# One decoder step on one core: the decode requests' heads move beside the delta rule, and prompt attention gets a block of its own

## The chip, the cores and the metric

The kernel runs on one core of a Trainium2 chip. The metric is the device time of one launch in microseconds (us). TensorE (PE) multiplies matrices; VectorE (DVE), ScalarE (ACT) and GpSimd (POOL) work element by element; SyncE (SP) issues most DMAs. Each engine takes its own instructions in the order in which they are written, and semaphores hold an engine until another has done something. TensorE runs at 1.2 or 2.4 GHz; the profile's "PEclk" is the granted share of 2.4 GHz.

## What is computed

One layer of a hybrid decoder for a prompt of 2048 tokens and for 8 decode requests of one token each, with 8192 earlier tokens of each request in a paged cache. The 1024-wide mix is made of two groups of four heads of 128.

```python
proj = jnp.einsum('btd,de->bte', rms_norm(x, norm_mix), w_in)
o_gdn, gdn_buf, gdn_s = gdn_branch(qkv, z, a, b, ...)   # gated delta rule, state 128x128 per head
o_dsa = dsa_fn(l, q, k, v, iq, ik, iw)                  # attention over the 256 best tokens
x = x + jnp.einsum('bte,ed->btd', concat(o_gdn, o_dsa), w_out)
...

def dsa_attend(q_pos, q, iq, iw, ik_all, gather_kv, n_sel, rel_bias):
    rel = relu(einsum('bthd,bsd->bths', iq, ik_all))
    score = einsum('bths,bth->bts', rel, iw)              # 8 index heads of 64
    _, sel = lax.top_k(score, n_sel)                      # 256 tokens
    k_sel, v_sel = gather_kv(sel)
    logits = einsum('btkgd,btskd->btkgs', qg, k_sel) * HEAD_DIM ** -0.5 + bias
    p = softmax(where(valid, logits, -inf))
    o = einsum('btkgs,btskd->btkgd', p, v_sel)
```

The layer ends with a causal convolution of three tokens over an up projection and a gated down projection.

Both parts do this: the prompt part for 2048 queries, the sample part for 8 requests against 8193 keys each, with one step of the delta rule for each request.

## The kernel before

The program is a row of blocks; a block ends on all engines before the next begins. `project`, `keys` and `channels` project the tokens; `channels` also makes the prompt's choice of 256 tokens and leaves it in DRAM as `left`. Then come, in this order, the five blocks that the change touches:

- `rule_and_attention` (names `mid_`): the delta rule for the prompt (`Delta`) and the prompt's attention (`Attention`), written into one stream for each engine. Before the rule, `Gates` prepares the decays.
- `delta_step` (`dstep_`): one step of the rule for the 8 requests, 32 states of 128x128.
- `step_select` (`pick_`): scores of 8192 cached index keys of each request, then a search for the 256th best score bit by bit, in 33 rounds.
- `step_slots` (`slot_`): turns the chosen tokens into lists of cache rows by one-hot matmuls.
- `step_attend` (`satt_`): gathers keys and values by indirect DMA and attends.

After them `mix`, `ffn_up` and `ffn_down` close the layer; they are not changed.

**The rule.** `Delta` takes the 16 chunks of 128 tokens as 8 pairs, `b` = 0 and 1 (buffers `A[b]`, `B[b]` in PSUM). A pair has an early stage (`sums`, `rows`, turns, `gram`), then 6 levels of a triangular inverse, then a late stage (`wt`, `vnew`, `kv`, `kvo`, output). A level writes on TensorE 4 products of `atm` and `x` (L2517) for each chunk, which ACT copies to `y` (L2610), and 4 products for `x` (L2526) and 4 for `xt` (L2529), which DVE subtracts (L2748, L2750). In the last level the product for `x` is left out. An f32 product is two MATMULs in the trace, so the six levels of a pair are 96 + 80 + 96 = 272 MATMULs of 64 columns, and a whole pair has 472.

**Attention.** `Attention` goes through 64 steps, a tile of 128 queries times a head. Step s does q·k in groups of 512 keys (L2177) with the mask added by a bf16 product (L2179), ACT copies each group out of PSUM (L2254), DVE adds the near bias (L2344) and takes the maximum (L2345), ACT takes the exponential (L2268). Two steps later TensorE turns the probabilities (L2192), ACT copies them (L2263), and TensorE multiplies them by v (L2228). q·k has two PSUM buffers, the turned probabilities have one. The tiles 0 to 3 have one group, 12 to 15 have four.

**What sets the order.** Each stage of the rule calls `side.spend(w)` with a weight that is written down by hand. `Beside` then advances the other stream until its share of its own total weight is as large as the rule's share. So the two are interleaved evenly by weight on every engine, and nothing at run time changes that order. The weights of the rule add up to 104.2 for a pair.

## Time and profile before

| what | us |
|---|---|
| median of 3 runs (4658.73 to 4661.22) | 4660.68 |
| the profiled execution's own time | 4658.32 |
| its span, first to last instruction | 4657.1 |
| block of rule and attention (1262 to 2343) | 1081 |
| four blocks of the sample part (2343 to 2823) | 480 |

The span is the execution that the rows below come from; it is 3.6 us under the median. The mean granted clock over it was 0.884. In a stretch the busy columns say for how long an engine had an instruction in work, with the count in brackets. A busy TensorE can be busy at half clock, so its busy time is read together with PEclk.

### The profile page before, as it was taken

To read this page: it belongs to the slowest core of one execution; us is meant where nothing else is said; L and a number is where in the kernel's file an instruction comes from. 1 tells how busy PE (TensorE), PEld (TensorE's weight loads), DVE (VectorE), ACT (ScalarE), POOL (GpSimd) and SP (SyncE) were. 2 spreads that over 40 slices of the span, in tenths; PEclk is the share of its full clock that TensorE was granted. 3 is DMA by queue.
4 is the path that set the end of the run, shared out by engine and by line. 5 is a ranking of instruction groups with operands and counts; after the bars stand their busy time and mean duration, and the time that the engine had idled before them with its cause. 6 is when DMAs were issued, how large, how long until landed. Compare 5 with 4: busy or idle time off the path is not lost. (4 is left out here: it accounts for less than half of the span.)

```text
span 4657.1 us, 51408 instructions
## 1 busy us (share of the span) xinstructions
PE 3985.0 (86%) x19290; PEld 3182.1 (68%) x19290; DVE 2136.5 (46%) x4206; ACT 1528.2 (33%) x2435; POOL 691.7 (15%) x547
## 2 busy tenths in 40 slices
PE   7788888888588888988859348989999999979999
PEld 4444454445287777877749334459999999958877
DVE  5538989898834433433322651224444444430200
ACT  2125565565434444544402001112222222221211
POOL 0100000000032222221200020111111111124443
PEclk9889899999768889989955557999999999989999
DMA  2242222120211111101031013311111111145433
GB/s 90 82 105 58 73 53 64 44 63 23 72 57 36 49 36 39 32 21 33 3 119 72 0 37 109 108 56 44 48 55 36 55 36 55 45 127 178 129 105 117
DMA packets 287233, 298.37 MB, mean 64 GB/s; under 512 B 33999, under 2 KB 231503, under 8 KB 282026
## 3 DMA queue, kind: packets, MB, share of 16 engines
q1 hardware_dynamic: 271822, 256.80, 19.2%
q0 software_dynamic: 2112, 20.97, 1.2%
q10 hardware_dynamic: 13120, 18.25, 1.2%
q8 instruction: 107, 1.75, 0.2%
q14 instruction: 72, 0.59, 0.0%
HBM read 202.16 MB, written 94.10 MB: 64 GB/s over the span
## 5 line engine op out<-in xcount | busy, mean ns | idle before, releaser
L530 PE MATMUL chan_p_g<-ht,chan_w 128*128 128x412 f32 (+1 forms) x1760 | 678.3, 529 | 62.7 <-ACT chan_flat L578 33.7
L1568 PE MATMUL up_p_g<-ht_high,up_wh 128*128 128x412 f32 (+1 forms) x1760 | 617.7, 351 | 0.3 <-POOL up_wl L1614 0.3
L1568 PE MATMUL up_p_g<-ht_high,up_wl 128*128 128x412 f32 (+1 forms) x1760 | 615.2, 350 | 0.0
L1568 PE MATMUL up_p_g<-ht_low,up_wh 128*128 128x412 f32 (+1 forms) x1760 | 615.2, 350 | 0.0
L530 PEld LDWEIGHTS chan_p_g<-ht,chan_w 128*128 128x128 f32 x1760 | 341.9, 197 | 310.5 <-issue 230.7
L1586 ACT ACTIVATE up_pre<-up_p_g 128x412 f32<-128x412 f32 (+1 forms) x220 | 113.6, 516 | 748.9 <-PE up_p_g L1568 748.9
L1948 ACT ACTIVATE chan_signed<-chan_sc,chan_trial 128x512 bf16<-128x512 f32 (+6 forms) x224 | 305.2, 1362 | 148.4 <-DVE chan_trial L2003 127.7
L1568 PEld LDWEIGHTS up_p_g<-ht_high,up_wh 128*128 128x128 f32 x1760 | 331.5, 188 | 1.9 <-issue 0.7
L1568 PEld LDWEIGHTS up_p_g<-ht_low,up_wh 128*128 128x128 f32 x1760 | 331.4, 188 | 1.2
L1568 PEld LDWEIGHTS up_p_g<-ht_high,up_wl 128*128 128x128 f32 x1760 | 331.2, 188 | 0.5
L1638 DVE TENSOR_SCALAR up_acc<-up_pre,up_taps 128x2048 f32<-128x2048 f32 x44 | 59.3, 1347 | 574.9 <-ACT up_pre L1586 574.9
L1989 DVE TENSOR_SCALAR_CACHE_REDUCE chan_tie<-chan_sc,chan_trial 128x384 bf16<-128x384 f32 (+6 forms) x224 | 316.2, 1412 | 7.5
L1806 PE MATMUL down_p_y<-down_wl,down_ah 128*128 128x512 f32 x704 | 274.4, 390 | 0.0
L1805 PE MATMUL down_p_y<-down_wh,down_ah 128*128 128x512 f32 x704 | 274.3, 390 | 0.0
L1807 PE MATMUL down_p_y<-down_wh,down_al 128*128 128x512 f32 x704 | 274.2, 389 | 0.0
L1924 PE MATMUL chan_p_sc<-ik,chan_iq 128*128 128x512 f32 (+3 forms) x304 | 185.9, 615 | 100.8 <-ACT chan_r L1943 90.6
L1777 POOL TENSOR_TENSOR down_al<-down_a,down_ah 128x1024 fp32r<-128x1024 f32 x88 | 211.7, 2406 | 359.0 <-ACT down_ah L1751 359.0
L1390 PE MATMUL mix_p_y<-mix_w,mix_m 128*128 128x512 f32 x544 | 238.9, 598 | 19.0 <-DMA mix_m<-scratch_mix 19.0
L1614 POOL TENSOR_TENSOR up_wl<-up_w,up_wh 128x1024 fp32r<-128x1024 f32 x44 | 128.8, 2928 | 839.6 <-ACT up_wh L1580 831.1
L1943 ACT ACTIVATE chan_r<-chan_p_sc 128x512 f32<-128x512 f32 (+3 forms) x304 | 159.7, 544 | 221.7 <-PE chan_p_sc L1925 115.4
L1751 ACT ACTIVATE down_ah<-down_a 128x1024 fp32r<-128x1024 f32 x88 | 93.4, 1061 | 385.9 <-PE down_p_y L1807 373.9
L1390 PEld LDWEIGHTS mix_p_y<-mix_w,mix_m 128*128 128x128 f32 x544 | 103.2, 192 | 143.3 <-issue 143.3
(521 smaller groups left out, 6962.2 us busy)
## 6 DMA issues: line engine op xcount, KB each, us to landing
down_a<-scratch_act SPq DMA_DIRECT2D x88, 512.0 KB, 3.6
scratch_act<-up_acc SPq DMA_DIRECT2D x22, 1028.0 KB, 5.2
up_w<-in_w_up SPq DMA_DIRECT2D x44, 512.0 KB, 6.4
chan_iq<-scratch_iq SPq DMA_DIRECT2D x28, 512.0 KB, 7.1
scratch_qkv<-chan_acc SPq DMA_DIRECT2D x12, 1028.0 KB, 4.6
mid_raw<-scratch_qkv SPq DMA_DIRECT2D x16, 768.0 KB, 5.4
chan_w<-in_w_in SPq DMA_DIRECT2D x22, 512.0 KB, 4.4
proj_x<-in_x_prompt SPq DMA_DIRECT2D x16, 512.0 KB, 3.6
```

Source lines behind the costliest of these rows:

```text
L530: last = pe.matmul(p_g[u % BANKS][:, 0:cols.stop - cols.start], weights[:, k, :], K.ht[:, k, cols], start=(k == 0), stop=(k == KD - 1))
L1390: last = pe.matmul(p_y[b][:, half, :], m[b][:, k, :], w[:, k, half * 512:(half + 1) * 512], start=(k == 0), stop=(k == KD - 1))
L1568: last = pe.matmul(p_g[u][:, 0:cols.stop - cols.start], wp[s][:, k, :], hp[:, k, cols], start=(k == 0 and m == 0), stop=(k == KD - 1 and m ...
L1614: pool.tensor_tensor(wl[s][:, :, :], w[s][:, :, :], wh[s][:, :, :].bitcast(F32), ALU.subtract).then_inc(s_wl[s], 1)
L1777: pool.tensor_tensor(al[t % RING][:, :, :], a[t % RING][:, :, :], ah[t % RING][:, :, :].bitcast(F32), ALU.subtract)\
L1805: pe.matmul(bank[0:m, :], hi, wh[:, f, :], start=(f == 0), stop=False)
L1806: pe.matmul(bank[0:m, :], hi, wl[:, f, :], start=False, stop=False)
L1807: last = pe.matmul(bank[0:m, :], lo, wh[:, f, :], start=False, stop=(f == NF - 1))
L1924: pe.matmul(out, self.iq[b][:, 0, h, :], self.K.ik2[:, cols], start=True, stop=False)
L1943: act.activation(self.r[n % self.RING][:, 0:width], self.p_sc[n % 2][:, 0:width], ACT.Relu).then_inc(S["relu"], 1)
L1948: act.activation(self.signed[:, 0:nk], self.sc[1][:, 0:nk], ACT.Sign, scale=-1.0, bias=self.trial[:, 1:2].bitcast(F32), accum_out=self.sig ...
L1989: last = dve.tensor_scalar(self.tie[:, 0:na], self.sc[0][:, 0:na], trial[:, 0:1].bitcast(F32), None, ALU.is_ge, ALU.add, accum_out=count[: ...
```

## The change

The four blocks of the sample part are gone as blocks. A class `Sample` writes the same work as a stream of steps with weights for each engine, in five parts: scoring (64 units of 4 transposes and 4 products), rule step (21 steps), search (35), slots (13) and attention (26). `heads` puts this stream beside the rule, over all eight pairs, where prompt attention stood; the prompt's attention, unchanged in its order, follows in a block of its own (`att_`) with nothing beside it. The sample stream weighs 6 + 171.6 + 42 + 84 + 65 + 62.4 = 431. The index pages of the first two pairs of requests are fetched before the rule starts. Slots are built in halves of 64 columns. Otherwise the sample part computes what it computed, in as many units and rounds.

```diff
-    def total(self):
+    def total(self, pairs):
...
-        return self.N * (early + (LEVELS - 1) * (self.W_YV + self.W_PROD) + late)
+        return 2 * len(pairs) * (early + (LEVELS - 1) * (self.W_YV + self.W_PROD) + late)
...
-    def tensor(self, pe, side):
+    def tensor(self, pe, side, pairs):
...
-        for j in range(self.N // 2):
+        for j in pairs:
...
+class Sample:
...
+    W_PREP, W_SCORE, W_RULE, W_SEARCH, W_SLOT, W_ATTEND = 3.0, 2.6, 2.0, 2.4, 5.0, 2.4
...
+    RULE_STEPS, SLOT_STEPS, ATTEND_STEPS = 21, 13, 26
+
+    def total(self):
+        return (2 * self.W_PREP + (self.UNITS + 2) * self.W_SCORE + self.RULE_STEPS * self.W_RULE + (self.ROUNDS + 2) * self.W_SEARCH
+                + self.SLOT_STEPS * self.W_SLOT + self.ATTEND_STEPS * self.W_ATTEND)
...
+    def tensor(self, pe):
+        yield from self.prepare_tensor(pe)
+        yield from self.score_tensor(pe)
+        yield from self.rule_tensor(pe)
+        yield from self.search_tensor(pe)
+        yield from self.slot_tensor(pe)
+        yield from self.attend_tensor(pe)
...
+    def vector(self, dve):
+        yield from self.prepare_vector(dve, step)
+        yield from self.score_vector(dve)
+        yield from self.rule_vector(dve, step)
+        yield from self.search_vector(dve, step)
+        yield from self.slot_vector(dve, step)
+        yield from self.attend_vector(dve, step)
...
+    def score_tensor(self, pe):
+        K, S, bank = self.K, self.S, self.bank
+        for step in range(self.UNITS + 2):
+            u = step
+            if u < self.UNITS:
+                i = u // self.PER
+                if u % self.PER == 0:
+                    pe.wait_ge(K.s_page[i % 2], i // 2 * 16 + 16)
+                if u >= 2:
+                    pe.wait_ge(S["copy"], u - 1)
+                for k in range(4):
+                    last = pe.transpose(bank[u % 2][:, k * P:(k + 1) * P], self.pages[i % 2][:, u % self.PER * 4 + k, :], K.ident[:, :])
+                last.then_inc(S["turn"], 1)
+            u = step - 1
+            if 0 <= u < self.UNITS:
+                if u == 0:
+                    pe.wait_ge(S["bd"], 1)
+                    pe.wait_ge(S["wread"], 1)
+                pe.wait_ge(S["copy"], u + 1)
+                if u >= 2:
+                    pe.wait_ge(S["mul"], u - 1)
+                for k in range(4):
+                    last = pe.matmul(bank[2 + u % 2][:, k * 32:(k + 1) * 32], self.turned[u % 2][:, k, :],
+                                     self.bd[:, u // self.PER, :, :, :].rearrange("p k q h -> p (k q h)"), start=True, stop=True)
+                last.then_inc(S["score"], 1)
+            yield self.W_SCORE
...
+    def search_tensor(self, pe):
+        K, S, bank = self.K, self.S, self.bank
+        for m in range(self.ROUNDS):
+            pe.wait_ge(S["row"], m + 1)
+            pe.matmul(bank[0][:, 0:PAIRS], K.halves[:, :], self.row[:, :], start=True, stop=True).then_inc(S["total"], 1)
...
+    def search_vector(self, dve, step):
...
+        def tally(level):
+            dve.tensor_tensor(nhit[:, :], sn[:, :], level, ALU.is_ge)
+            step(dve.tensor_tensor(hit[:, :, :], s[:, :, :], level.unsqueeze(2).broadcast_to(wide), ALU.is_ge))
+            dve.tensor_reduce(row[:, :], hit[:, :, :], AX.X, ALU.add).then_inc(S["row"], 1)
+
+        def too_few(m):
+            dve.wait_ge(S["total"], m + 1)
+            step(dve.tensor_tensor(count[:, :], bank[0][:, 0:PAIRS], nhit[:, :], ALU.add))
+            step(dve.tensor_scalar(miss[:, :], count[:, :], float(NSEL), None, ALU.is_lt))
...
+            tally(trial[:, :].bitcast(F32))
+            yield self.W_SEARCH
+            too_few(31 - bit)
+            step(dve.scalar_tensor_tensor(out=trial[:, :], in0=miss[:, :], scalar=bit, in1=other[:, :],
+                                          op0=ALU.logical_shift_left, op1=ALU.bitwise_xor))
...
+def heads(nc, K, ins, outs):
+
+
+    with phase(nc, "rule") as (c_rule, stack_rule):
+        rule = Delta(c_rule, K, ins["gdn_out_norm"].rearrange("l (p o) -> (l p) o", o=1), outs["p_gdn"].rearrange("h k v -> k h v"))
+        with phase(nc, "step") as (c, stack):
+            few = TILES * GH
+            gate = Gates(c, K, ins["gdn_a_log"], ins["gdn_dt_bias"], rule.A[0][:, 0, 0:few], rule.B[0][:, 0, 0:few])
+            sample = Sample(c, K, ins, outs)
+            pairs = range(NT // 2)
+            beside = lambda stream: Beside(stream, sample.total(), rule.total(pairs))
+            block = open_block(nc, stack, c)
+
+            @block.sync
+            def _(sp):
+                gate.sync(sp)
+                rule.sync(sp, beside(sample.sync(sp)), pairs)
+                sample.finished(sp)
+
+            @block.tensor
+            def _(pe):
+                gate.tensor(pe)
+                rule.tensor(pe, beside(sample.tensor(pe)), pairs)
+
+            @block.scalar
+            def _(act):
+                gate.scalar(act)
+                rule.scalar(act, beside(sample.scalar(act)), pairs)
+
+            @block.gpsimd
+            def _(pool):
+                gate.gpsimd(pool)
+                sample.begin(pool)
+                pool.wait_ge(gate.S["g"], 1)
+                rule.gpsimd(pool, beside(sample.gpsimd(pool)), pairs, gate.S["ready"])
+
+            @block.vector
+            def _(dve):
+                gate.vector(dve)
+                dve.wait_ge(gate.S["ready"], 1)
+                rule.vector(dve, beside(sample.vector(dve)), pairs)
+
...
+    with phase(nc, "att") as (c, stack):
         att = Attention(c, K)
-        beside = lambda stream: Beside(stream, att.total(), rule.total())
+        alone = lambda stream: Beside(stream, att.total()).rest()
...
         def _(pe):
-            gate.tensor(pe)
-            rule.tensor(pe, beside(att.tensor(pe)))
+            alone(att.tensor(pe))
...
-                rule_and_attention(nc, K, ins["gdn_a_log"], ins["gdn_dt_bias"], ins["gdn_out_norm"].rearrange("l d -> (l d)"), outs)
-                delta_step(nc, K, ins["state_gdn"].rearrange("l b h k v -> (l b) h k v"),
-                           ins["gdn_out_norm"].rearrange("l d -> (l d)"), dict(outs, s_gdn=outs["s_gdn"].rearrange("(b h) k v -> b h k v", h=GH)))
...
-                step_select(nc, K, ins["cache_idx_k"].rearrange("l n p d -> (l n) p d"), ins["page_table"])
...
-                step_slots(nc, K, ins["page_table"])
-                step_attend(nc, K, ins["cache_k"], ins["cache_v"], ins["q_norm"].rearrange("l d -> (l d)"))
...
+                heads(nc, K, ins, outs)
```

**TensorE in the levels.** Before, the start of the levels of a rule pair; `mid_p_a` names are prompt attention, which sits between the rule's pieces:

```order
L2517 MATMUL mid_p_A<-mid_x,mid_atm 128x64 x4
L2177 MATMUL mid_p_a_l<-mid_a_kt,mid_a_qg 128x512
L2179 MATMUL mid_p_a_l<-mid_a_left,mid_a_shut 128x512
L2517 MATMUL mid_p_A<-mid_x,mid_atm 128x64 x4
L2526 MATMUL mid_p_B<-mid_y,mid_xt 128x64 x4
L2529 MATMUL mid_p_B<-mid_xt,mid_y 128x64 x4
L2192 MATMUL mid_p_a_t<-ident,mid_a_lg 128x128 x4
L2177 MATMUL mid_p_a_l<-mid_a_kt,mid_a_qg 128x512
L2179 MATMUL mid_p_a_l<-mid_a_left,mid_a_shut 128x512
L2526 MATMUL mid_p_B<-mid_y,mid_xt 128x64 x4
```

The same place in the first pair now (line numbers are those of the changed file); `step_` names are the sample part, here its scoring:

```order
L1866 MATMUL rule_p_A<-rule_x,rule_atm 128x64 x8
L1875 MATMUL rule_p_B<-rule_y,rule_xt 128x64 x4
L1878 MATMUL rule_p_B<-rule_xt,rule_y 128x64 x4
L2515 MATMUL step_p_s<-ident,step_pages 128x128 x4
L2526 MATMUL step_p_s<-step_bd,step_turned 128x32 x4
L1875 MATMUL rule_p_B<-rule_y,rule_xt 128x64 x4
L1878 MATMUL rule_p_B<-rule_xt,rule_y 128x64 x4
L1866 MATMUL rule_p_A<-rule_x,rule_atm 128x64 x8
L2515 MATMUL step_p_s<-ident,step_pages 128x128 x4
```

Where wide products of attention stood between the rule's 64-column products there are now 4 transposes and 4 products of 32 columns.

**VectorE in the search.** Before, a round of the search is written alone, in `step_select`:

```order
L973 TENSOR_REDUCE pick_row<-pick_hit 128x4
L975 TENSOR_TENSOR pick_count<-pick_p_c,pick_nhit 128x4
L987 TENSOR_SCALAR pick_miss<-pick_count 128x4
L988 SCALAR_TENSOR_TENSOR pick_trial<-pick_miss,pick_other 128x4
L983 TENSOR_SCALAR pick_other<-pick_trial 128x4
L971 TENSOR_TENSOR pick_nhit<-pick_sn,pick_trial 128x4
L972 TENSOR_TENSOR pick_hit<-pick_s,pick_trial 128x512
```

Now it stands between the rule's subtractions of the levels:

```order
L2099 TENSOR_TENSOR rule_x<-rule_x,rule_p_B 128x128x2
L2101 TENSOR_TENSOR rule_xt<-rule_xt,rule_p_B 128x128x2
L2699 TENSOR_TENSOR step_count<-step_p_s,step_nhit 128x4
L2700 TENSOR_SCALAR step_miss<-step_count 128x4
L2715 SCALAR_TENSOR_TENSOR step_trial<-step_miss,step_other 128x4
L2709 TENSOR_SCALAR step_other<-step_trial 128x4
L2693 TENSOR_TENSOR step_nhit<-step_sn,step_trial 128x4
L2694 TENSOR_TENSOR step_hit<-step_s,step_trial 128x512
L2695 TENSOR_REDUCE step_row<-step_hit 128x4
L2099 TENSOR_TENSOR rule_x<-rule_x,rule_p_B 128x128x2
L2101 TENSOR_TENSOR rule_xt<-rule_xt,rule_p_B 128x128x2
```

and on TensorE the product that the round waits for stands between the rule's products:

```order
L1866 MATMUL rule_p_A<-rule_x,rule_atm 128x64 x8
L1875 MATMUL rule_p_B<-rule_y,rule_xt 128x64 x4
L1878 MATMUL rule_p_B<-rule_xt,rule_y 128x64 x4
L2678 MATMUL step_p_s<-step_row,halves 128x4
L1875 MATMUL rule_p_B<-rule_y,rule_xt 128x64 x4
L1878 MATMUL rule_p_B<-rule_xt,rule_y 128x64 x4
L1866 MATMUL rule_p_A<-rule_x,rule_atm 128x64 x4
L2678 MATMUL step_p_s<-step_row,halves 128x4
```

A round's count (L2678 on TensorE) waits for the DVE row above (L2695) that is written at the same place of the rule, and the rule's next products stand behind it.

**TensorE in the block of attention alone.** Now, a step of a tile with two groups of keys:

```order
L1523 MATMUL att_p_a_l<-att_a_kt,att_a_qg 128x512
L1525 MATMUL att_p_a_l<-att_a_left,att_a_shut 128x512
L1538 MATMUL att_p_a_t<-ident,att_a_lg 128x128 x4
L1523 MATMUL att_p_a_l<-att_a_kt,att_a_qg 128x256
L1525 MATMUL att_p_a_l<-att_a_left,att_a_shut 128x256
L1538 MATMUL att_p_a_t<-ident,att_a_lg 128x128 x2
L1574 MATMUL att_p_a_o<-att_a_v,att_a_pt 128x128 x6
```

The same pieces as before follow one another without the rule's between them.

## Rows read from the trace of the kernel before

**Rows 1.** Busy time by stage: the rule block, then the sample blocks.

```profile
core 0 of [0], span 4657.1 us
core 0: us, PE busy (x) PEld busy (x) DVE busy (x) ACT busy (x) POOL busy (x), PEclk, DMA share, GB/s
1262.00:2343.00 1081.00, 920.63 (x6086) 803.63 (x6086) 409.01 (x926) 477.30 (x837) 257.79 (x291) 0.86 0.13 37
2343.00:2823.00 480.00, 278.13 (x1625) 259.45 (x1625) 191.18 (x560) 48.67 (x83) 38.48 (x42) 0.51 0.16 54
```

**Rows 2.** The same columns: scoring, slots, pair 1, its levels, levels of pair 3.

```profile
2417.00:2590.00 173.00, 160.70 (x774) 158.88 (x774) 39.84 (x154) 38.27 (x64) 1.88 (x2) 0.50 0.19 76
2681.00:2746.00 65.00, 28.50 (x522) 27.46 (x522) 51.18 (x95) 0.00 (x0) 3.44 (x5) 0.61 0.02 3
1281.80:1424.40 142.60, 123.08 (x669) 113.35 (x669) 53.08 (x152) 59.58 (x124) 36.82 (x40) 0.68 0.17 50
1320.90:1396.80 75.90, 73.28 (x364) 69.03 (x365) 21.54 (x63) 24.59 (x56) 22.59 (x27) 0.57 0.10 29
1589.90:1650.20 60.30, 55.51 (x407) 49.38 (x407) 23.59 (x46) 24.12 (x45) 20.97 (x26) 0.92 0.06 16
```

**Rows 3.** TensorE groups in the levels of pair 1.

```profile
L2529 PE MATMUL mid_p_B<-mid_xt,mid_y 128*128 128x64 f32 x96 | 19.4, 370 | 0.0
L2517 PE MATMUL mid_p_A<-mid_x,mid_atm 128*128 128x64 f32 x96 | 19.3, 376 | 4.5 <-DVE mid_xt L2739 4.5
L2526 PE MATMUL mid_p_B<-mid_y,mid_xt 128*128 128x64 f32 x80 | 17.2, 389 | 0.0
```

**Rows 4.** TensorE in order of time, levels of pair 1: start, length.

```profile
1341.88 1.91 PE L2526 MATMUL mid_p_B<-mid_y,mid_xt 128*128 128x64 f32 x8
1343.58 1.92 PE L2529 MATMUL mid_p_B<-mid_xt,mid_y 128*128 128x64 f32 x8
```

**Rows 5.** The same view in the levels of pair 3.

```profile
1629.22 1.08 PE L2177 MATMUL mid_p_a_l<-mid_a_kt,mid_a_qg 128*128 128x512 f32 x2
1630.13 0.38 PE L2179 MATMUL mid_p_a_l<-mid_a_left,mid_a_shut 128*128 128x512 bf16 x1
1630.35 1.00 PE L2526 MATMUL mid_p_B<-mid_y,mid_xt 128*128 128x64 f32 x8
1631.19 1.06 PE L2529 MATMUL mid_p_B<-mid_xt,mid_y 128*128 128x64 f32 x8
1632.08 0.61 PE L2192 MATMUL mid_p_a_t<-ident,mid_a_lg 128*128 128x128 f32 x4
1632.53 1.06 PE L2228 MATMUL mid_p_a_o<-mid_a_v,mid_a_pt 128*128 128x128 f32 x8
```

**Rows 6.** Groups while the sample part scores: names, count, busy, mean ns, idle.

```profile
L894 PE MATMUL pick_p_x<-pick_bd,pick_turned 128*128 x512 | 112.7, 386 | 0.0
L884 PE MATMUL pick_p_t<-ident,pick_pages 128*128 128x128 f32 x256 | 69.1, 429 | 9.9 <-DMA pick_pages<-in_cache_idx_k,pick_pid 9.9
```

**Rows 7.** All engines in order of time, one search round.

```profile
2641.42 0.59 PE L901 MATMUL pick_p_c<-pick_row,halves 128*128 128x4 f32 x2 [2.25 <-DVE pick_row L973]
2642.04 0.16 DVE L975 TENSOR_TENSOR pick_count<-pick_p_c,pick_nhit 128x4 f32<-128x4 f32 x1 [0.68 <-PE pick_p_c L901]
...
2644.25 0.58 PE L901 MATMUL pick_p_c<-pick_row,halves 128*128 128x4 f32 x2 [2.25 <-DVE pick_row L973]
```

**Rows 8.** The tile of attention's logits: count, duration min/median/max in ns.

```profile
L2254 ACT ACTIVATE mid_a_lg<-mid_p_a_l,mid_a_rq x160: 353/687/703, 1289.3 to 2298.3; 128x512 f32<-128x512 f32 x112, 128x128 f32<-128x128 f32 x16, 128x256 f32<-128x256 f32 x16, 128x384 f32<-128x384 f32 x16
L2344 DVE TENSOR_TENSOR mid_a_lg<-mid_a_lg,near x64: 281/419/1059, 1294.3 to 2301.7; 128x256 f32<-128x256 f32 x60, 128x128 f32<-128x128 f32 x4
L2345 DVE TENSOR_REDUCE mid_a_bias<-mid_a_lg x64: 286/1287/2287, 1294.7 to 2302.1; 128x1 f32<-128x128 f32 x4, 128x1 f32<-128x256 f32 x4, 128x1 f32<-128x384 f32 x4, 128x1 f32<-128x512 f32 x4
L2268 ACT ACTIVATE mid_a_lg<-mid_a_lg,mid_a_bias x64: 401/1202/2004, 1295.0 to 2304.4; 128x128 f32<-128x128 f32 x4, 128x256 f32<-128x256 f32 x4, 128x384 f32<-128x384 f32 x4, 128x512 f32<-128x512 f32 x4
```

**Rows 9.** ScalarE groups of the whole block: count, busy us, mean ns.

```profile
L2263 ACT ACTIVATE mid_a_pt<-mid_p_a_t 128x512 f32<-128x512 f32 (+3 forms) x160 | 84.7, 530 | 88.2 <-PE mid_p_a_t L2192 87.2
...
L2298 ACT ACT_TABLE_LOAD x16 | 20.5, 1283 | 0.3
```

More of the change, by code:

```diff
@@ L2570, in tensor, with scalar @@
         side.rest()
-    def scalar(self, act, side):
+    def scalar(self, act, side, pairs):
         S, A, B, st = self.S, self.A, self.B, self.st
-        for j in range(self.N // 2):
+        for j in pairs:
             for b in range(2):
@@ L2632, in scalar, with gpsimd @@
         side.rest()
-    def gpsimd(self, pool, side, ready):
+    def gpsimd(self, pool, side, pairs, ready):
         K, S = self.K, self.S
-        pool.memset(K.state[:, :, :], 0.0).then_inc(S["zero"], 1)
-        for j in range(self.N // 2):
+        if 0 in pairs:
+            pool.memset(K.state[:, :, :], 0.0).then_inc(S["zero"], 1)
+        for j in pairs:
             for b in range(2):
@@ L2682, in gpsimd, with vector @@
         side.rest()
-    def vector(self, dve, side):
+    def vector(self, dve, side, pairs):
         K, S, A, B, st = self.K, self.S, self.A, self.B, self.st
-        step = Chain(dve, S["step"])
-        dve.wait_ge(S["gain"], 16)
-        dve.wait_ge(S["zero"], 1)
-        for j in range(self.N // 2):
+        step = Chain(dve, S["step"], self.steps)
+        if 0 in pairs:
+            dve.wait_ge(S["gain"], 16)
+            dve.wait_ge(S["zero"], 1)
+        for j in pairs:
             for b in range(2):
@@ L2783, in vector @@
         side.rest()
+        self.steps = step.n
 class Gates:
@@ L2880, in _ @@
         def _(sp):
-            gate.sync(sp)
-            rule.sync(sp, beside(att.sync(sp)))
+            alone(att.sync(sp))
             att.finished(sp)
```

1320 lines of the change are left out of this document (701 added, 619 removed).

## The prediction, made before the changed kernel was run

> **What bounds the kernel now.** Read the busy time by stage first [rows 1]. The stretch that the change rewrites is 1081 us of rule and prompt attention and 480 us of sample part, 1561 of the span's 4657.1. In the first block TensorE is busy for 921 of 1081 us at a mean granted clock of 0.86, and no other engine for more than 477. So TensorE is the bound there. In the sample blocks no engine is: TensorE has 278 us, DVE 191, and they wait for one another. That is the 480 us the change can win, and it wins them only if TensorE has room beside the rule for 278 us.
>
> Read the clock next, since TensorE's busy time hangs on it. In the levels of pair 3, with attention of two key groups between them, the granted clock is 0.92 and 407 MATMULs take 60.3 us. In the levels of pair 1, where attention's tiles are at most four blocks wide, it is 0.57, and 364 MATMULs take 75.9 us, though TensorE is busy for 73.3 of them [rows 2]. While the sample part scores, TensorE is busy for 160.7 of 173 us and the clock is 0.50 throughout. So a full queue doesn't by itself give 2.4 GHz in this kernel.
>
> Then the price of one small product at either level. In pair 1, 8 MATMULs of 64 columns start 1.70 us before the next 8, which is 0.213 us each [rows 4]. In pair 3 it is 0.84 to 0.89 us for 8, 0.105 to 0.111 each [rows 5]. It doubles at half clock.
>
> **The change part by part.** I compare 1561 us with three terms: a head, the rule with the sample part beside it, and attention alone.
>
> *Head.* Gates and first loads take 20 us before pair 1 starts at 1281.8; they stay. The index pages' DMAs are issued before the rule and are hidden by this, or cost what the sample part waited for its first page, at most 10 us [rows 6].
>
> *The clock in the levels.* The changed levels have scoring units or nothing wide between them. Both neighbours that the trace shows, rule levels with narrow attention and scoring alone, ran at or near 1.2 GHz [rows 2]. I take 1.2 GHz for the levels of all pairs. The rule's own 272 MATMULs of the levels then need 272 x 0.213 = 58 us a pair; the three groups of pair 1 show 55.9 busy [rows 3]. At 2.4 GHz they would need 30.
>
> *Pairs beside scoring.* Scoring is 178 of the stream's 431 weight, so it fills 3.3 of the 8 pairs, 64/3.3 = 19 units or 233 MATMULs a pair. Pair 1 is the nearest row: 669 MATMULs, 472 of the rule and 197 of attention, in 142.6 us at a clock of 0.68 [rows 2]. 3.3 x 142.6 = 471 us.
>
> *Pairs without scoring.* From pair 1 I take out what attention put into its levels, 75.9 - 55.9 = 20 us, and an estimated 10 us for what it held up in the early and late stage (its table loads of 1.28 us [rows 9] stand between the rule's square roots and exponentials). That leaves 112 us, and 4.7 x 112 = 526 us. The bounds: 104 us, all 472 MATMULs at 0.213 with the 16 wide ones at double, and 123, the pair without the second deduction.
>
> *Search.* Here the change adds a wait. A round's count product on TensorE waits for the DVE reduction that stands at the same place of the rule. A round now lasts 2.83 us from product to product, of which 2.2 is DVE's part, from the count at 2642.04 to the next product at 2644.25 [rows 7]. Behind the waiting product on TensorE are the rule's next products, and ACT, DVE and POOL wait for those. DVE gets to its place only after its subtraction, so the whole 2.2 us are often exposed after the level's second products, and less after its first ones. I take 2.2 for each: 33 x 2.2 = 73 us. Bounds: 0 and 33 x 3.5 = 115, with the subtractions' 0.8 us and handing over added.
>
> *Rule step, slots, sample attention.* The trace of before has them alone only. Their TensorE work is small beside 112 us a pair, but it is added while TensorE is the bound: about 20, 20 and 22 us, from 29, 27 and 37 us of products at half clock of which about half lies in levels, with DVE pieces of 4 to 5 us (slots keep DVE busy for 51 of 65 us [rows 2]) ahead of the rule's subtractions. Together 62 us, between 20 and 110. POOL's gathers (38 us in all [rows 1]) stand between the rule's masks and are hidden, since POOL was busy for a quarter of the block; with that cover gone they cost those 38.
>
> The loads and stores of the sample part go through SP's queue between the rule's; SP waits there only for things that the other engines have passed at the same place. Three block ends fewer are inside the 480 us.
>
> First block: 20 + 471 + 526 + 73 + 62 = 1152 us.
>
> *Attention alone.* Nothing hides its chain now. Take a step of tiles 12 to 15, four groups. On TensorE a group costs 1.13 us for q·k with its mask (1629.22 to 1630.35), 0.45 for four transposes and 0.89 for eight products with v [rows 5]: 2.4 us. Call the end of the last q·k X. ACT copies it out (0.69), DVE adds the bias (0.42) and takes the maximum (up to 2.29), ACT takes the exponential (up to 2.0, and 0.19 to read the sum) [rows 8]: X + 6.2 with handing over. ACT takes its engine's instructions in order, so the next step's first group is copied out and its transposes copied only then (0.69 + 0.6 [rows 8, 9]), X + 7.5. TensorE has meanwhile used its two PSUM buffers and waits for the single buffer of turned probabilities, though it had work for only 3.5 us. Then it does one transpose set, two sets of v products and two q·k groups, and the next X is 12.4 us after the last. By the same count a step with three groups takes 8.7 us, with two 5.3, with one 3.0. 16 x (12.4 + 8.7 + 5.3 + 3.0) = 470. Each tile adds two table loads on ACT (1.28 each), a square, a root and a copy, about 4.5 us of which I take 3.8: 60 us. 530 us. Bounds: 430, if the tables and half of the waits at the last group overlap; 600, if the waits also cost the clock.
>
> *Sum.* 1152 + 530 = 1682 against 1561: +121 us. The profiled execution of before took 4658.3, 2.4 us under the median. 4658.3 + 121 = 4779, and I say 4780.
>
> **A rule of the skill on the clock.** Pair 1 has a clock of 0.57 at 73.3 busy of 75.9 us [rows 2]. The Trainium skill, "TensorE: Matmul & The Clock Gate", section "HAM oscillation — how this bites in real kernels", holds that what costs the clock is idle gaps, and that a TensorE kept busy stays at full rate. By that rule the levels, which have no gaps, would run at 2.4 GHz, and the time would be that of rival A. The two rows of this trace speak against it, so it stands as a rival with a small chance.
>
> **Rivals.**
>
> A. *The levels keep 2.4 GHz.* The dense stretches before them (`gram`, the transposes) raise the clock and the levels hold it. For it: pair 3's levels ran at 0.92. Against: those had wide attention products between them, and pair 1's did not hold it. Then the levels are bound by the chain of product, copy, product, subtraction, an estimated 5.7 us each (48 products at 0.11 and a handing over), 34 us a pair instead of 58; scoring's 19 units lose half of their share in the levels too, 7 us. 3.3 x 31 + 4.7 x 24 = 215 us less: 4565, faster than before. It decides from where the levels' clock is above about 0.8 on average, which gives back the 121 us.
>
> B. *Attention alone runs at the pace of its busiest engine.* Its parts may overlap better than my chain says, since three logits buffers are there. ACT's share is 160 copies of up to 0.69 us, 160 of 0.53, 64 exponentials of 1.2 [rows 8, 9] and the tables and squares, some 340 us; TensorE's is about 350 by the spacings of [rows 5]. 400 us instead of 530 gives 4650, no change. Against: the one buffer of turned probabilities ties TensorE to ACT in every group.
>
> C. *DVE's pieces all come ahead of the rule.* The sample part's 191 us of DVE [rows 1] stand in line before the subtractions. If most are exposed and not only the search's, add 80 us: 4860.
>
> D. *The sample stream doesn't run beside the rule,* since its waits make every step one after another. It would cost up to the old 480 us less what is hidden; TensorE's order of rows makes this unlikely, and I put it within C.
>
> **How the numbers follow.** Forecast (slower, about 4780) 0.70, rival A 0.13, B 0.09, C and D 0.08. The forecast's own bounds: search -73 to +42, pairs -38 to +52, other parts -42 to +48, attention -100 to +70; not all at one end, so about 4665 to 4880. The range of 4630 to 4880 leaves out A and a part of C. Two medians of this kernel can be told apart from about 0.2%, 9 us. Faster by more: A and half of B, 0.18. Within: 0.04. Slower: 0.78.
>
> **What would show it.** In the profile after: the rule block about 1150 us long and the block of attention about 530. The granted clock in the levels at 0.5 to 0.6 in the pairs beside scoring, with products of the levels 0.21 us apart; a level stretch near 1.0 would be rival A. TensorE waiting for the search's reduction about 2 us, 33 times. In the block of attention, ACT waiting for the maximum in nearly every step, and TensorE waiting for ACT's copy of the turned probabilities; steps of the last tiles 12 us apart. I am wrong in the main if pairs take about 110 us beside scoring, or if attention needs 430 us or less.

## The result and the profile after

The changed kernel takes 4845.18 us (median of 4 runs, 4843.66 to 4845.86). Against before the ratio is 1.0397, with a 95% interval of 1.0381 to 1.0412: 184.6 us slower, where 121 were forecast. The profiled execution has a span of 4844.6 us.

Busy time by stage, the view of [rows 1]: the rule block, the block of attention alone, the eight pairs of the rule one by one, and the levels of pair 1.

```profile
core 0: us, PE busy (x) PEld busy (x) DVE busy (x) ACT busy (x) POOL busy (x), PEclk, DMA share, GB/s
1262.00:2491.00 1229.00, 977.06 (x5407) 936.24 (x5407) 478.85 (x1214) 216.23 (x377) 284.28 (x317) 0.61 0.13 39
2491.00:3013.00 522.00, 405.12 (x2304) 291.37 (x2304) 145.49 (x304) 309.56 (x543) 25.27 (x16) 0.90 0.12 34
1282.00:1427.60 145.60, 131.20 (x696) 128.94 (x697) 43.10 (x129) 31.15 (x55) 35.32 (x46) 0.62 0.27 101
1427.60:1569.70 142.10, 133.27 (x726) 131.44 (x725) 42.72 (x116) 32.42 (x58) 29.81 (x35) 0.63 0.15 49
1569.70:1709.90 140.20, 130.64 (x713) 128.44 (x714) 39.73 (x112) 32.33 (x56) 29.06 (x34) 0.63 0.06 17
1709.90:1852.10 142.20, 129.86 (x620) 118.59 (x620) 51.77 (x113) 25.81 (x46) 36.30 (x34) 0.61 0.12 34
1852.10:2023.90 171.80, 111.72 (x516) 104.71 (x516) 77.04 (x222) 21.93 (x37) 29.17 (x34) 0.56 0.11 31
2023.90:2179.70 155.80, 107.00 (x567) 101.87 (x567) 83.92 (x206) 20.99 (x36) 28.97 (x34) 0.57 0.06 14
2179.70:2338.30 158.60, 105.75 (x939) 98.96 (x938) 85.47 (x179) 22.03 (x39) 57.68 (x58) 0.68 0.15 41
2338.30:2482.00 143.70, 126.50 (x638) 122.33 (x637) 46.40 (x107) 23.20 (x43) 36.89 (x40) 0.58 0.04 12
1317.90:1399.90 82.00, 79.69 (x381) 79.58 (x382) 15.82 (x47) 10.03 (x21) 15.49 (x20) 0.51 0.00 1
```

What was 1561 us in [rows 1] is now 1229 + 522 = 1751. The four pairs beside scoring are alike, 140 to 146 us. The longest are pairs 5 and 6, where the search runs, and TensorE is *less* busy there (107 to 112 us) than beside scoring: these pairs wait. The clock of the first block fell from 0.86 to 0.61, and in the levels of pair 1 it is 0.51 with TensorE busy for 79.69 of 82.0 us.

TensorE in order of time in those levels, to be read beside [rows 4] and [rows 5]: 8 products start 1.71 us after the last 8, the spacing of half clock.

```profile
1341.55 1.91 PE L1875 MATMUL rule_p_B<-rule_y,rule_xt 128*128 128x64 f32 x8
1343.26 1.91 PE L1878 MATMUL rule_p_B<-rule_xt,rule_y 128*128 128x64 f32 x8
1344.96 1.06 PE L2515 MATMUL step_p_s<-ident,step_pages 128*128 128x128 f32 x4
```

One search round in pair 6, all engines in order of time (rows that repeat a step left out), as in [rows 7]. The last figure in brackets is the idle time ahead of the row.

```profile
2087.66 1.70 PE L1878 MATMUL rule_p_B<-rule_xt,rule_y 128*128 128x64 f32 x7
...
2089.39 0.42 DVE L2099 TENSOR_TENSOR rule_x<-rule_x,rule_p_B 128x256 f32<-128x256 f32 x1 [2.66 <-PE rule_p_B L1878]
2089.72 0.41 DVE L2101 TENSOR_TENSOR rule_xt<-rule_xt,rule_p_B 128x256 f32<-128x256 f32 x1
2090.06 0.15 DVE L2699 TENSOR_TENSOR step_count<-step_p_s,step_nhit 128x4 f32<-128x4 f32 x1
...
2091.51 0.69 DVE L2695 TENSOR_REDUCE step_row<-step_hit 128x4 f32<-128x512 f32 x1
...
2092.26 0.59 PE L2678 MATMUL step_p_s<-step_row,halves 128*128 128x4 f32 x2 [2.90 <-DVE step_row L2695]
...
2092.70 3.65 PE L1866 MATMUL rule_p_A<-rule_x,rule_atm 128*128 128x64 f32 x16
```

TensorE's last product of the level ends at 2089.36. DVE first does the rule's two subtractions, then the whole round, and TensorE stands for 2.90 us until it may count; the rule's next products (L1866) stand behind. In the view of waits of pairs 5 to 8 (us in total, times, longest) it is TensorE's largest. The second row below is a wait that a rule pair alone doesn't have: the 12.4 us in it are one slot step of DVE that is written ahead of the rule's `rule_vb` in pair 7.

```profile
PE step_p_s L2678 <- DVE step_row L2695: 88.3, 27, 7.5
...
PE rule_p_A L1847 <- DVE rule_vb L2063: 14.0, 2, 12.4
```

The block of attention, by the number of key groups in a step (one, two, three, four; 16 steps each), and two of its waits:

```profile
2506.10:2564.20 58.10, 41.82 (x202) 30.01 (x203) 22.84 (x73) 39.15 (x88) 6.50 (x4) 0.79 0.19 55
2564.20:2649.80 85.60, 72.76 (x454) 51.74 (x453) 32.39 (x77) 64.47 (x121) 6.26 (x4) 1.00 0.17 51
2649.80:2793.70 143.90, 117.49 (x691) 83.65 (x690) 41.42 (x77) 90.26 (x152) 6.26 (x4) 0.95 0.09 27
2793.70:3013.00 219.30, 169.67 (x949) 123.08 (x947) 47.38 (x75) 113.00 (x179) 3.13 (x2) 0.88 0.06 17
```

```profile
ACT att_a_lg L1614 <- DVE att_a_bias L1691: 80.7, 55, 2.4
...
PE att_p_a_t L1538 <- ACT att_a_pt L1609: 37.5, 26, 3.3
```

ACT waits for the maximum in 55 of 64 steps, and TensorE waits for the copies of the turned probabilities: the chain that the prediction drew.

### The profile page after: what moved, and what is told of

It reads as the page before. It is cut to its first block and busy times, and to the rows that moved or that the text cites. A ratio compares the mean times of both kernels' runs of the same rounds, so it can differ in the third digit from the quotient of the medians.

```text
span 4844.6 us, 51064 instructions
## 1 busy us (share of the span) xinstructions
PE 4167.8 (86%) x19290; PEld 3346.5 (69%) x19290; DVE 2160.5 (45%) x4238; ACT 1527.6 (32%) x2435; POOL 705.0 (15%) x547
```

## The experiments

Theory 1: the levels are long because they run at 1.2 GHz. Theory 2: the search costs the wait of a product for a reduction at the same place. Their rivals: the levels are bound by their chain, or can't hold 2.4 GHz; and DVE's own pieces cost the time. Times are compared as ratios to before, since before itself took 4646.6 us on the chip of the first four runs (`shift`, `kick`, `alone`, `swap`) and 4659.4 and 4659.3 us on those of the others. That chip differs in one more thing, which bears on several comparisons; it is told under `again` and `later`.

**`shift`: the count product one step later.**

```diff
     def search_tensor(self, pe):
         K, S, bank = self.K, self.S, self.bank
+        yield self.W_SEARCH
         for m in range(self.ROUNDS):
...
         yield self.W_SEARCH
-        yield self.W_SEARCH
```

> One edit: the count product of a search round on TensorE stands one step of the sample stream later than the DVE reduction that it waits for; the same work in total. In the changed kernel TensorE waits 88 us for that reduction in pairs 5 to 8. Theory (the wait of products at the same place, put at 73 us in the prediction): the waits of TensorE for step_row fall below 10 us, pairs 5 and 6 go from 172 and 156 us to about 130 each, and the whole kernel is 60 to 90 us shorter, about 4770 us. Rival (DVE's own pieces, in line ahead of the rule's subtractions, make these pairs long, and the wait only shows it): TensorE waits for the rule's subtractions instead, pairs 5 and 6 stay above 150, and the kernel gains at most 20 us.

Measured: 4760.28 us, ratio 1.0237 (1.0220 to 1.0254), 1.5% or 71 us under the changed kernel. The windows of pairs 5 to 8:

```profile
1853.40:1979.70 126.30, 100.06 (x514) 96.85 (x513) 79.62 (x217) 21.73 (x37) 29.59 (x34) 0.62 0.14 38
1979.70:2112.40 132.70, 103.81 (x571) 100.19 (x570) 89.81 (x212) 21.17 (x37) 29.38 (x34) 0.60 0.08 21
2112.40:2248.40 136.00, 101.77 (x937) 95.05 (x937) 85.20 (x179) 21.92 (x39) 54.29 (x54) 0.73 0.15 41
2248.40:2392.90 144.50, 125.75 (x639) 121.43 (x637) 45.99 (x106) 23.19 (x43) 40.62 (x44) 0.59 0.06 18
```

Pair 5 fell by 45.5 us and pair 6 by 23.1: 68.6 us in all for the wait. TensorE's wait for step_row fell to 29.9 us in 9 times, not below 10 as the theory said; 15.4 us of it are in pair 5. Theory 2 holds for these pairs. Pair 7 fell by 22.6 us too, though no search runs there; more on that under `again` and `later`. The eight pairs lose 90 us, the two profiled spans differ by 81: the blocks behind took 7 us longer here.

**`kick`: wide products before the levels.** Nobody reads them; they are extra work in the time in which TensorE waits for the rule's first masks.

```diff
                 last.then_inc(S["syst"], 1)
                 side.spend(self.W_SYS)
+            self.kick(pe, j)
             for l in range(1, LEVELS):
...
+    kicks = 4
+
+    def kick(self, pe, j):
+        for _ in range(self.kicks):
+            pe.matmul(self.B[1][:, :, :], self.K.ident[:, :], self.K.below[:, 0:512], start=True, stop=True)
```

> One edit: between the last transposes of the early stage and the levels, where TensorE stands idle for 5 to 14 us in every pair, it makes 4 products of 128x512 that nobody reads (8 MATMULs, 0.45 us each at 2.4 GHz, 0.9 at 1.2). Added work, none removed. Theory (the levels cost 80 us a pair because they run at 1.2 GHz, and they keep the higher level if they enter at it): granted clock in the levels 0.9 or more, levels 50 us instead of 80, pairs beside scoring 142 to about 115, whole kernel 100 to 200 us shorter. Rival 1 (the products of the levels don't hold 2.4 GHz in any case): the clock falls back to 0.5 within the first levels, and the kernel is 0 to 30 us longer. Rival 2 (the levels are bound by the chain product, copy, product, subtraction, so the clock is of no use to them): clock up, levels still above 70 us.

Measured: 4694.48 us, ratio 1.0092 (1.0047 to 1.0137), some 3% under the changed kernel, but the runs lie between 4663.8 and 4737.1 us. The trace is of the longest. Levels of pairs 1 and 2:

```profile
1319.90:1363.00 43.10, 42.60 (x383) 42.27 (x382) 13.93 (x43) 10.03 (x21) 15.11 (x20) 1.00 0.01 2
1419.50:1498.90 79.40, 78.60 (x394) 78.52 (x393) 15.50 (x45) 10.64 (x22) 17.38 (x23) 0.53 0.13 54
```

The same six levels with nearly the same products (383 and 394 MATMULs) take 43.1 us at 1.00 and 79.4 at 0.53, and TensorE is busy for 99% of either. Pair 1's own levels took 82.0 at 0.51 in the changed kernel. So the clock is the price of the levels beside scoring, and the chain of the rule is not. But they hold 2.4 GHz only in some pairs: theory 1 is right on the cause, and rival 1 on most of the pairs: 1 and 3 stayed up, 2 fell as its levels began, and 4 to 8 lie between 0.53 and 0.81.

**`alone`: three blocks with nothing beside one another.**

```diff
+            none = lambda: Beside(iter(()), 0.0, rule.total(pairs))
...
-                rule.tensor(pe, beside(sample.tensor(pe)), pairs)
+                rule.tensor(pe, none(), pairs)
...
+        whole = lambda stream: Beside(stream, sample.total()).rest()
...
+            whole(sample.tensor(pe))
```

> Three blocks with nothing beside one another: the rule, then the sample part, then prompt attention. It measures the terms of the sum. The prediction's term: a pair of the rule alone takes 112 us (104 to 123) at a clock near 0.5, so the rule's block is 20 + 8 x 112 = 916 us; the sample part alone about the old 480 us; attention 522 as measured. Together about 5010 us. If the miss of some 76 us in the first block comes from the term for pairs without scoring, a pair alone takes 122 us or more; if it comes from the sample part's pieces, it takes 112 or less.

Measured: 4993.04 us, ratio 1.0743. The rule's block, the sample part's, attention's, then pair 4 and its levels:

```profile
1262.00:2183.00 921.00, 761.93 (x3780) 732.30 (x3780) 261.77 (x618) 173.67 (x297) 230.26 (x275) 0.62 0.09 24
2186.00:2636.00 450.00, 277.44 (x1627) 260.11 (x1627) 192.74 (x591) 48.38 (x83) 37.52 (x42) 0.51 0.17 57
2636.00:3155.00 519.00, 407.81 (x2304) 294.14 (x2304) 145.76 (x306) 311.20 (x544) 25.29 (x16) 0.90 0.11 33
1617.30:1730.00 112.70, 95.10 (x475) 91.39 (x474) 31.85 (x74) 21.25 (x37) 28.60 (x34) 0.62 0.09 24
1647.30:1707.50 60.20, 58.13 (x273) 58.00 (x274) 11.41 (x25) 4.64 (x12) 16.31 (x22) 0.50 0.00 1
```

A pair alone takes 112.7 us, so that term was right, and the miss lies in the sample part's pieces. They take 450 us alone and 1229 - 921 = 308 beside the rule: the change hides 142 us of them, and pays for it with attention's 519. Beside the rule, attention had cost only 1081 - 921 = 160 us, what it did to the clock included.

**`again` and `later`: what stood still in pair 7.** In the changed kernel's trace, DVE and ACT crawl in the late stage of pair 7 while POOL issues the gathers of keys and values. DVE's 32 MEMSETs of one column take 10.2 us: 18 of them 0.30, the rest mostly one every 0.7 us (the first rows of that stretch). ACT starts L1970 15 us after its input, which was done at 2307.7.

```profile
2303.76 0.30 DVE L2932 MEMSET step_starts<- 128x1 f32 x18
2304.41 0.95 POOL L2427 DMA_INDIRECT step_kg<-in_cache_k,row  x1 [0.30 <-issue]
2304.82 0.09 DVE L2932 MEMSET step_starts<- 128x1 f32 x2 [0.76 <-issue]
2305.54 0.06 DVE L2932 MEMSET step_starts<- 128x1 f32 x1 [0.64 <-issue]
...
2323.10 0.60 ACT L1970 ACTIVATE rule_at<-rule_p_B 128x512 f32<-128x512 f32 x1 [19.70 <-remote]
```

In `shift` the same 32 MEMSETs, also among gathers, took 0.44 us:

```profile
2233.10 0.44 DVE L2932 MEMSET step_starts<- 128x1 f32 x31
```

> The changed kernel itself, once more. In its first trace DVE and ACT stood nearly still from 2303 to 2323 us, in the late stage of pair 7, while POOL issued 24 gathers; pair 7's late stage took 51 us there and 28.6 us in the trace of the run shift, whose DVE and ACT instructions are the same. If it belongs to this program, the late stage is again about 51 us and the time again 1.0397 of before; if it was an accident of one execution, the late stage is about 28 us while the time is about the same or 20 us shorter.

`again` is the changed kernel unchanged: 4841.81 us, ratio 1.0391; pair 7's late stage again 51.5 us. It was no accident of one execution. But the chip is a rival here that no run took up. `shift`, `kick`, `alone` and `swap` ran on one chip, and none of these four traces lists a wait that the profile puts down to "remote", as in the ACT row above. Each of the ten other traces has such waits among the gathers, the trace of before too (ACT, 12.8 us the longest). On the one chip before took 13 us less as well. (The chip of the changed kernel's first trace isn't on record; before took 4660.6 us there, as on the others.) So the comparison with `shift` doesn't show that the program decides; the same program was not traced on both kinds of chip.

`later` ran on a chip that shows these waits. It puts POOL's gathers four steps on, with a count DELAY of 4:

```diff
+        for _ in range(self.DELAY):
+            yield self.W_ATTEND
         pool.wait_ge(S["slots"], 1)
...
-        for _ in range(self.ATTEND_STEPS - 2 * QUARTERS):
+        for _ in range(self.ATTEND_STEPS - 2 * QUARTERS - self.DELAY):
```

> The changed kernel with POOL's 32 gathers four steps of the sample stream later, which is about 0.2 of a pair, so that they fall into the early stage of pair 8 and not into the late stage of pair 7. Theory (the gathers as they are placed hold DVE and ACT up in the late stage): pair 7's late stage 28 us and no stall anywhere, 20 us shorter than the changed kernel, 4820 us. Rival 1 (the stall goes where the gathers go): pair 8's early stage 20 us longer, no gain. Rival 2 (the stall belongs to that place in the program, not to the gathers): pair 7's late stage again 51 us.

Measured: 4832.88 us, ratio 1.0373, 9 us under `again`, not 20. Pair 7 and pair 8:

```profile
2180.20:2318.70 138.50, 103.00 (x938) 96.30 (x938) 84.62 (x179) 21.98 (x39) 42.72 (x42) 0.72 0.12 31
2318.70:2470.70 152.00, 124.84 (x638) 120.51 (x637) 43.78 (x107) 23.20 (x43) 52.26 (x56) 0.60 0.09 25
```

Pair 7 lost 20 us, its MEMSETs taking 0.44 us, and pair 8 got 8 longer. The edit moved fewer gathers than was meant: 8 of the 32 still ran in pair 7's late stage (from 2289.67 on), where the changed kernel has 24, and a short wait remained there (DVE L2110 starts 1.7 us later than in `shift`, counted from the first gather). In pair 8 POOL's masks stand behind the moved gathers: its second mask starts 48.2 us into the pair, against 38.2 before the edit. So on a chip that shows the stall, it was nearly gone with 8 gathers there instead of 24. What holds DVE and ACT up stays open.

**`bothhold`: a wide product in each level as well.** `shift` and `kick`, and after the two sets of first products of a level:

```diff
                     last.then_inc(S["yv"], 1)
                     side.spend(self.W_YV)
+                pe.matmul(self.B[1][:, 0:4, :], self.K.ident[:, :], self.K.below[:, 0:512], start=True, stop=True)
                 for b in range(2):
```

> The changed kernel with three edits: the count product one step later (as in shift), 4 unread products of 128x512 before the levels (as in kick), and one unread product of 128x512 in each of the 6 levels, after the two sets of first products. In kick the levels of pairs 1 and 3 ran at 1.00 throughout and took 43 us, and those of pair 2 fell back to 0.5 as they began. Theory (narrow products hold 2.4 GHz only from time to time, wide ones between them hold it always): clock in all levels 0.95 or more, levels 45 to 50 us in all eight pairs, the kernel 200 to 250 us shorter than shift, about 4530 us, and the runs close together. Rival (what decides is an accident of timing, wide products or not): the clock still falls back in some pairs, and the time is that of shift plus 8 x 5 us of added products less what some pairs gain, 4650 to 4750.

Measured: 4639.49 us, ratio 0.9953 (0.9937 to 0.9970). Levels of pair 1 took 48.2 us at 1.00, but those of pair 4, where the rule step's narrow products stand between, 73.6 at 0.63; over the eight pairs the clock lies between 0.61 and 1.00. The time is under the rival's 4650 to 4750 and far from the theory's 4530: wide products help more often, and not always. Still, with these edits the changed arrangement is 20 us *faster* than before.

**`swap`, `swapkick`, `swaphold`: the other pairing.** The rule alone in a block, and the sample part beside attention, whose waits are there to be filled. `swap` adds no product, `swapkick` those of `kick`, `swaphold` those of `kick` and the one in each level.

```diff
+            def both(stream, other):
+                side = Beside(other, sample.total(), att.total())
+                for w in stream:
+                    side.spend(w)
+                side.rest()
...
+                both(att.tensor(pe), sample.tensor(pe))
```

> The rule alone in a block of its own, and the sample part beside prompt attention in the next. Forecast from the windows: the rule 916 us; attention alone is 522 us with TensorE busy for 405, so TensorE has about 117 us idle there, and the sample part's 278 us of TensorE work at 1.2 GHz would be about 150 at the clock of 0.9 that attention has. If the two fill each other's waits, the second block takes 560 to 650 us, and the kernel 4845 - 1229 - 522 + 916 + 600 = 4610 us. Rival (the sample part's waits stand in line and add as they do beside the rule, 0.8 of its 480 us): second block about 900 us, kernel about 4910.

> The rule alone in its block with the 4 unread products of 128x512 before the levels, the sample part beside prompt attention (as in swap, where the rule's levels took 60.2 us a pair at 0.50). Theory: where the clock holds, the levels are bound by the chain product, copy, product, subtraction, an estimated 34 us from 8 products at 0.107 us each and the handing over; 8 pairs x 26 us less than swap is 4480. If it falls back in half of the pairs, as in kick, about 4580. If the added products only cost their time (8 x up to 7 us), 4690 to 4745.

> As swapkick, and one unread product of 128x512 in each level as well, after the two sets of first products (0.9 us each at 2.4 GHz, 1.8 at 1.2). Theory: the clock holds in all levels, they take 34 us and up to 5 us for the added products, about 4515 us and steady. Rival (they stand in the chain and the clock falls back all the same): 6 x 1.8 us x 8 pairs = 86 us more than swapkick.

Measured: `swap` 4690.61 us, ratio 1.0092 (1.0072 to 1.0113); `swapkick` 4717.22, ratio 1.0129 (1.0112 to 1.0146); `swaphold` 4558.27, ratio 0.9772 (0.9754 to 0.9791). The second block of `swap` and its end from the first gather on:

```profile
2184.00:2850.00 666.00, 560.48 (x3931) 444.42 (x3931) 332.80 (x900) 352.80 (x625) 65.36 (x58) 0.91 0.20 64
2745.30:2850.00 104.70, 90.67 (x610) 73.84 (x609) 34.41 (x110) 51.30 (x83) 32.84 (x32) 0.95 0.16 47
```

The rule's block of `swaphold`, its second block and the end of that from the first gather on, then the levels of pairs 4 and 2:

```profile
1262.00:2017.00 755.00, 617.05 (x3940) 543.86 (x3940) 264.54 (x618) 173.80 (x297) 227.30 (x275) 0.86 0.11 29
2020.00:2725.40 705.40, 580.33 (x3931) 457.70 (x3931) 332.76 (x900) 354.58 (x625) 63.31 (x58) 0.87 0.19 60
2593.50:2725.40 131.90, 95.88 (x621) 77.03 (x619) 34.37 (x110) 52.82 (x85) 30.61 (x32) 0.86 0.13 37
1594.50:1633.60 39.10, 36.84 (x286) 33.32 (x287) 10.85 (x25) 4.65 (x12) 16.13 (x22) 1.00 0.01 1
1403.50:1448.90 45.40, 43.17 (x286) 39.12 (x286) 10.87 (x25) 4.66 (x12) 16.17 (x22) 0.85 0.00 1
```

Beside attention the sample part costs 666 - 519 = 147 us, beside the rule 308; in these 308 are the 69 us of the search's wait that `shift` took away and the 23 of the stall in pair 7. `shift`, which has neither and ran on the chip of `swap` and `alone`, comes to 219 (1140 - 921). Where the 303 us that attention hides (519 + 450 - 666) come from can be read from TensorE: 178 are idle time (111 and 173 alone, 106 together), and 125 are busy time (408 and 277 alone, 560 together), as the sample part runs at 0.91 there and not at 0.51. Still, `swap` without added products is not faster than before, and its second block lies 16 us over the forecast's 650.

In `swapkick` the products ahead of the levels were of no use: the clock there was 0.53 and the levels 59.5 us. With one wide product in each level as well they took 39 to 45 us, and the block 755 instead of 920. The second block grew from 666 to 705 us with nothing in it changed, 39 of the 43 us by which `swaphold` came out over the forecast. From the first gather to the block's end it takes 131.9 us instead of 104.7, with TensorE idle for 36 instead of 14 and waits on "remote" among the gathers: 27 of the 39 us arise there, 22 of them idle time: the stall again, on another chip than `swap`. `swapkick` has it too, with 32 MEMSETs in 6.5 us. The other 12 us go with a clock of 0.87 instead of 0.90 up to the first gather.

**`inlevels`: `swaphold` without the four products ahead.**

> swaphold without the 4 products before the levels; only the one unread product of 128x512 in each level stays. It tells whether the levels need to be entered at 2.4 GHz. If they do: clock 0.5 in the levels, 60 us and the added products at half clock, up to 71 us a pair, 4558 + 8 x 28 = 4780. If wide products inside them are enough: about 41 us a pair as in swaphold, 4550 to 4570.

Measured: 4588.25 us, ratio 0.9852 (0.9837 to 0.9868). Levels of pairs 3 and 4:

```profile
1501.00:1542.30 41.30, 39.01 (x285) 34.92 (x286) 11.19 (x25) 4.65 (x12) 16.13 (x22) 0.92 0.01 2
1592.30:1638.30 46.00, 45.08 (x285) 40.54 (x286) 10.42 (x25) 4.65 (x12) 16.51 (x22) 0.80 0.00 1
```

The time is 18 us over the second case and far from the first: the levels need not be entered at 2.4 GHz. With the wide product in them they ran at 0.80 to 0.92 in all eight pairs. The four ahead are worth another 30 us.

**`final`: `swaphold` with the count product one step later.**

> The kernel of swaphold with the count product one step later, as in shift. In swaphold the sample part beside attention made a second block of 705 us, against 519 for attention alone. Theory (the wait at the same place costs beside attention what it costs beside the rule, about 70 us in shift): second block about 640 us, kernel about 4490 us. Rival (attention's own waits hide it there): no more than 15 us shorter than swaphold, about 4545.

Measured: 4557.23 us, ratio 0.9778 (0.9765 to 0.9792), the same as `swaphold`. TensorE's wait for step_row had been 34.5 us there and is 13.3 here; the block went from 705 to 699. Beside attention, this wait is hidden. The rival was right.

**`oldhold`: the kernel before with the same products in pair 1 alone.**

> The kernel before, with the added products in pair 1 alone (4 of 128x512 before its levels and one in each level). Its levels took 75.9 us at 0.57 there, and 60.3 us at 0.92 in pair 3 with more MATMULs. Theory (its levels too are slow only by the clock): clock in pair 1's levels 0.95, levels 50 to 55 us, kernel 15 to 25 us shorter than before, about 4638 us. Rival: no gain, since attention's other work then is not hidden, within 9 us of before.

Measured: 4639.30 us, ratio 0.9956 (0.9943 to 0.9970), 20 us shorter, as the theory said, though with levels at 0.85 and not 0.95. Whether the arrangement of before, with such products in all its pairs, would reach `swaphold` was not tried. The levels of pair 1 went from 75.9 us at 0.57 [rows 2] to:

```profile
1323.90:1382.00 58.10, 56.83 (x376) 50.70 (x376) 20.23 (x60) 22.95 (x54) 22.56 (x27) 0.85 0.14 40
```

## Why the prediction was right, and where 64 us more came from

**The clock in the levels** was read rightly: 0.50 to 0.51 in seven of eight pairs, 0.72 in pair 7. `kick` shows that this is what they cost. The Trainium skill, "TensorE: Matmul & The Clock Gate", section "HAM oscillation — how this bites in real kernels", speaks of idle gaps as what costs the clock. The rows here speak against it as the whole cause: TensorE was busy for 79.69 of 82.0 us at 0.51, and for 42.60 of 43.1 at 1.00 with the same products. Rival A fell with it, though its price was fair: at 2.4 GHz the levels beside scoring are 39 us shorter (82.0 to 43.1), where I had put 31.

**Pairs beside scoring**: forecast 142.6, measured 145.6, 142.1, 140.2. **A pair of the rule alone**: forecast 112, measured 112.7. **The search's wait**: forecast 73, and one step more between the two took away 68.6; that isn't all of it, as the next part shows. **Attention alone**: forecast 530, measured 522, in part by luck: steps of one to four groups took 3.6, 5.4, 9.0 and 13.7 us with their share of tables, roots and copies, where my sum has 4.0, 6.3, 9.7 and 13.4, which is 23 us too much in all; and the 15 us before the first step (2491 to 2506.1) were not in my sum. Rival B's 400 us were far off.

**The mis-sized term is what the sample part adds beyond its scoring and the search's wait.** The prediction gave it 62 us, with 110 as the upper bound. Against 112.7 us for a pair alone, with `shift` for what is not the wait:

| piece | forecast, us | measured, us |
|---|---|---|
| rule step | 20 | 21: 0.7 of pair 4's excess of 29.5 |
| search, beyond what `shift` took away | 0 | 22: pair 5 of `shift` 13.6, and 0.64 of that in pair 6 |
| slots | 20 | 31: rest of pair 6, 0.85 of pair 7's 23.3 |
| sample attention | 22 | 35: pair 8's 31.8 and the rest of pair 7 |
| DVE and ACT standing still in pair 7 | 0 | 23: 158.6 - 136.0 |
| end of the sample part behind pair 8 | 0 | 7: 2482 to 2491, less the 2 us that the block of `alone` has there |
| together | 62 | 139 |

The shares of pairs follow from the stream's weights. Four things failed in that step, each for another reason.

- The search costs 69 + 22 = 91 us, 2.75 a round and not 2.2. That is nearly all its wait: TensorE waited 88.3 us for the reduction in these pairs, and of the 22 us that `shift` left, 15.4 stand in pair 5 alone as the same wait, longer than that pair's excess of 13.6. DVE does the rule's subtractions first and then the round, which I had put into the upper bound only.
- Sample attention is TensorE's own work. In pair 8 TensorE is busy for 126.5 us instead of the 95.1 of a pair alone, and idle for 17.2 instead of 17.6. I had taken 22 us for 37 us of products, as if those outside the levels ran at 2.4 GHz; over that pair the clock was 0.58.
- Slots I had counted by TensorE's work, while here DVE's pieces are what the rule waits for: in pair 7 of `shift` TensorE is idle for 34.2 us instead of 17.6, and 12.4 of that is one wait for `rule_vb` behind a slot step. That much of rival C is true, though its "all of them exposed" is not.
- I called the gathers hidden because POOL had room, and looked at POOL's queue alone; what suffered was DVE and ACT. The size of 23 us is a comparison across chips, and its cause is open.

These readings are from the traces; only the search's wait was taken away by an edit.

The sum: 77 us more in that table, 6 more for 0.7 us in each pair, 4 less for the search's wait and 2 less for scoring make the first block 77 us longer than forecast (1229 against 1152). Attention alone took 8 less. 121 + 77 - 8 = 190, which is 1751 - 1561. The medians differ by 184.6: the blocks behind took 1831.6 us (4844.6 - 3013) instead of 1834.1, and before's median of 4660.6 lies 3.5 us over its profiled span, the new one 0.6.

## What to carry to other kernels

Before small products are moved away from wide ones, read the granted clock of a stretch in which they stand without them: here that stretch was in the trace of before, and one wide product in each level, which nobody reads, bought back more than it cost (ratio 0.9772 with the sample part beside attention). Whether two streams go together is read from what both do to the busiest engine: the sample part cost 147 us beside attention, where TensorE's idle time was filled and the clock was 0.91, and 219 to 308 beside the rule alone at 0.61 to 0.63. A product that waits for a reduction of another engine belongs a step behind it, unless what it stands in has waits to spare.

## What the runs showed of the hardware that was not expected

- Nearly the same narrow products ran at either level of the clock for whole stretches: 43.1 us at 1.00 and 79.4 at 0.53 in one execution. Executions of one program then differ by up to 73 us (`kick`).
- One product of 128x512 in each level raised the clock of levels that ran at 0.50 without it (0.80 and 0.92 in `inlevels`). Four of them ahead of levels without such a product did nearly nothing with the rule alone (0.53 in `swapkick`), yet beside scoring two of three pairs held 1.00 (`kick`).
- Among gathers by indirect DMA, DVE took 10.2 us for 32 MEMSETs that take 0.44 otherwise, and ACT stood beside it. Waits of this kind are in all ten traces of the other chips, before's included, and in none of the four of the chip of `shift`, `kick`, `alone` and `swap`. In the sample part beside attention it is 27 us between `swap` and `swaphold`, whose second blocks have the same instructions. No run settles why.
